# Last stage of a gated decoder layer in two passes, with the output projection by seven block products

## The reference

```python
y_pool = multiscale_pool(u_pool, pool_w[l], pool_scale[l]) * jax.nn.silu(z_pool)
...
y_attn = attn.reshape(B, S, ATTN_WIDTH) * jax.nn.silu(z_attn)
gates = jax.nn.sigmoid(gate_logits + b_gate[l]).reshape(B, S, 2, D)
merged = (gates[:, :, 0] * jnp.einsum('bsp,pd->bsd', y_pool, w_pool_up[l])
          + gates[:, :, 1] * jnp.einsum('bsa,ad->bsd', y_attn, w_attn_up[l]))
x = x + jnp.einsum('bsd,de->bse', merged, w_out[l])
...
return rms_norm(x, final_g)
```

## Time and profile before

| what | value |
|---|---|
| median of 3 runs | 1636.92 us (1635.85 to 1638.66) |
| profiled execution, its own time | 1635.96 us |
| its span, first to last instruction | 1634.2 us |
| mean granted TensorE clock | 0.994 of full speed |
| PE, DVE, ACT, POOL busy, share of the span | 97%, 69%, 46%, 55% |
| DMA, mean over the span | 140 GB/s |

### The profile page before, as it was taken

One profiled execution on the slowest core, in us unless ns is written; L12 is line 12 of the kernel. 1 busy time (PEld: TensorE's weight loads), 2 busy tenths in 40 slices (PEclk: granted clock), 3 DMA queues, 4 the chain that ended last, 5 costly groups with the idle time before them and its releaser, 6 DMA issues. The chain is left out here.

```text
span 1634.2 us, 24931 instructions
## 1 busy us (share of the span) xinstructions
PE 1586.9 (97%) x8030; PEld 1321.3 (81%) x8030; DVE 1134.6 (69%) x1554; ACT 755.8 (46%) x1448; POOL 906.3 (55%) x665
## 2 busy tenths in 40 slices
PE   7999999999999999999999999999999899999998
PEld 5877888788888887888887888888887688888886
DVE  7745425764989889998998988999887763333323
ACT  4422222224667665676665666666666431112111
POOL 3421112421789878888777897898874332314140
PEclk9999999999999999999999999999999999999999
DMA  7742336754434243452793333434314773534332
GB/s 257 233 134 106 129 116 194 250 156 143 140 94 114 82 139 86 114 139 76 242 334 104 107 97 102 119 91 140 100 43 142 220 228 111 165 108 149 116 103 77
DMA packets 150868, 228.82 MB, mean 140 GB/s; under 512 B 46929, under 2 KB 72017, under 8 KB 150754
## 3 DMA queue, kind: packets, MB, share of 16 engines
q1 hardware_dynamic: 150754, 227.42, 45.3%
HBM read 149.76 MB, written 77.60 MB: 139 GB/s over the span
## 5 line engine op out<-in xcount | busy, mean ns | idle before, releaser
L1593 DVE TENSOR_TENSOR_SCAN left<-keep,left 128x512 f32<-128x512 f32 x192 | 297.1, 1547 | 33.5 <-issue 22.4
L1420 PE MATMUL psum<-hT,ring 128*128 128x512 f32 x644 | 264.5, 411 | 5.2 <-DVE sum_d L1629 2.3
L1660 POOL TENSOR_TENSOR ring<-raw,ring 128x512 fp32r<-128x512 f32 x138 | 232.9, 1688 | 60.2 <-ACT ring L1500 45.7
L1424 PE MATMUL psum<-hT,ring 128*128 128x512 f32 x644 | 263.2, 409 | 0.0
L1422 PE MATMUL psum<-hT,ring 128*128 128x512 f32 x644 | 262.6, 408 | 0.0
L1506 ACT ACTIVATE keep<-psum 128x512 f32<-128x512 f32 (+3 forms) x320 | 170.5, 533 | 178.5 <-PE psum L1446 176.5
L1513 ACT ACTIVATE wt<-psum 128x512 fp32r<-128x512 f32 (+3 forms) x320 | 170.9, 534 | 110.8 <-PE psum L1454 107.9
L1466 PEld LDWEIGHTS psum<-wt,vm 128*128 128x128 f32 x1088 | 171.6, 189 | 32.8 <-issue 7.0
L1599 DVE TENSOR_TENSOR wt<-psum,wt 128x512 fp32r<-128x512 f32 (+3 forms) x320 | 189.7, 593 | 8.4 <-ACT wt L1513 5.9
L1466 PE MATMUL psum<-wt,vm 128*128 128x256 f32 x1088 | 182.5, 282 | 5.1 <-DVE row_sum L1608 4.3
L1454 PE MATMUL psum<-ident,left 128*128 128x128 f32 x1088 | 170.8, 272 | 1.4 <-DVE wt L1599 1.3
(11 more groups left out here) (181 smaller groups left out, 3231.3 us busy)
## 6 DMA issues: line engine op xcount, KB each, us to landing
raw<-in_w_strips SPq DMA_DIRECT2D x92, 256.0 KB, 4.1
qm<-qk_scratch SPq DMA_DIRECT2D x128, 128.0 KB, 4.1
gate<-gate_scratch SPq DMA_DIRECT2D x64, 256.0 KB, 4.0
hT<-form_scratch SPq DMA_DIRECT2D x28, 512.0 KB, 8.1
xt<-in_x SPq DMA_DIRECT2D x16, 512.0 KB, 5.2
xT<-in_x_T SPq DMA_DIRECT2D x16, 512.0 KB, 4.1
qk_scratch<-staging SPq DMA_DIRECT2D x32, 256.0 KB, 2.7
qk_scratch<-store_lo SPq DMA_DIRECT2D x32, 256.0 KB, 3.6
```

What stands on the lines that cost most here:

```text
L1420: pe.matmul(o, hi, m_hi, start=k == 0, stop=False)
L1424: last = pe.matmul(o, lo, m_hi, start=False, stop=k == HK - 1)
L1593: dve.tensor_tensor_scan(left[:, n % LN, span][:, ::-1], k, k, carry, ALU.mult, ALU.bypass).then_inc(scanned, 1)
L1660: pool.tensor_tensor(out_, a, b, op).then_inc(s, 1)
```

## The change

Stage 4 is written anew, without hardware loops. It has two passes.

**Pass one** makes the 64 up-projections (`UPS`), for each chunk first the 8 tiles of the pooling branch, then the 8 of the attention branch. The gated pooling tile goes to `rows`, where the attention tile is added, and the sum is stored to a new DRAM scratch, `m_d`. Gate tiles have three buffers (`GN`), and a step n issues the load for step n + 2, which waits until the buffer of step n - 1 is free. Weight pieces have three slots and are now only those of the up-projections, pool's first. The output projection's weights are loaded in the second and third chunk; from their four quarters B11, B12, B21, B22 VectorE forms the sums T1 to T4, and every one of the seven factors (`FORMS`) is split in two parts.

**Pass two** takes the merged values back in 8 pairs of 128 tokens (256 tokens each, `OUT_PAIRS`), in two halves of the channels. Per pair GpSimd forms S1 to S4 (`make_forms`), ScalarE and VectorE split the seven factors into a ring of six, and PE makes seven products of 128 tokens by 512 output channels with 4 slices each (`out_part`, 12 matmuls). The results are put together from PSUM: two by copies on ScalarE, five by adds on VectorE, and six further adds on GpSimd (`join`) in SBUF. x is loaded straight into `rows`, and rows are normed and stored as before.

Two waits of stage 2 on VectorE and GpSimd are also named otherwise or dropped. The diff, cut to its core:

```diff
@@ class Opening @@
-    SLOTS, EARLY = 4, 3
+    SLOTS, EARLY = 3, 3
...
+        b, m = divmod(i, KT)
+        slot = self.raw[:, i % self.SLOTS, :].rearrange("p (k n) -> p k n", n=P)
+        sp.dma_start(slot, self.up[b][:, :, m * P:(m + 1) * P]).then_inc(self.raw_in[i % self.SLOTS], DMA)
@@ build @@
+    m_d = scratch("merged_scratch", [KT, P, SEQ])
@@ stage2 @@
-                                      hT[:, HOME[TURN[i]], kk, 0, :].bitcast(F32), ALU.subtract).then_inc(near_lo, 1)
+                                      hT[:, HOME[TURN[i]], kk, 0, :].bitcast(F32), ALU.subtract)
@@ stage4 @@
-            with pe.Fori(0, NC) as c:
...
-                for m, b in [(0, 0), (1, 0), (0, 1), (1, 1)] + [(m, b) for m in range(2, NM) for b in range(2)]:
-                    up(c, m, b)
...
-                for t in range(1, NT):
-                    for h in range(2):
-                        project(c, t, h, range(KT))
+    NM, UPS = KT, NC * 2 * KT
+    GN, RN, BANKS, AHEAD = 3, 6, 4, 5
+    OUT_PAIRS, PARTS = TT // 2, TT // 2 * FORMS
...
+    def up_of(n):
+        return n // (2 * NM), n // NM % 2, n % NM
+    def at_up(c, b, m):
+        return (2 * c + b) * NM + m
...
+    Y1_TURN = {3: 0, 4: 1, 6: 2, 7: 3}
...
         @block.sync
...
+            def load_gate(n):
+                c, b, m = up_of(n)
+                if n >= GN:
+                    c0, b0, m0 = up_of(n - GN)
+                    if b0 == 0:
+                        sp.wait_ge(gated, n - GN + 1)
+                    else:
+                        sp.wait_ge(summed, c0 * NM + m0 + 1)
+                sp.dma_start(gates[n % GN][:, :], gate_d[b * KT + m, :, tokens(c)]).then_inc(g_in[n % GN], DMA)
...
+            def load_mt(p):
+                if p % 2 == 0:
+                    for i in range(2):
+                        sp.wait_ge(m_stored[i], m_count(p // 2, NM - 2 + i))
+                if p == 0:
+                    sp.wait_ge(w_lo, wo_split(HK, 0))
+                    sp.wait_ge(wo_formed, 4 * HK)
+                    sp.wait_ge(y_lo_done[1], UK * NC)
+                elif p == 1:
+                    sp.wait_ge(up_done, UPS)
+                else:
+                    sp.wait_ge(s_lo, FORMS * (p - 1))
+                for kh in range(2):
+                    sp.dma_start(mt[p % 2][kh][:, :, :], m_d[kh * HK:(kh + 1) * HK, :, pair_tokens(p)].rearrange("k q t -> q k t")
+                                 ).then_inc(mt_in[p % 2], DMA)
...
+            load_gate(0)
             last_stores(sp)
+            load_gate(1)
+            for n in range(UPS):
+                c, b, m = up_of(n)
+                if n + EARLY < 2 * NM:
+                    load_up(n + EARLY)
+                if n + 2 < UPS:
+                    load_gate(n + 2)
+                if n == 4:
+                    load_z(0, 2)
+                    load_z(0, 3)
+                    for s, count in zip(sum_stored, SUM_STORES):
+                        sp.wait_ge(s, count * DMA)
+                    for s in y_stored:
+                        sp.wait_ge(s, PAIRS * 4 * DMA)
+                if m == 0 and b == 1 and c + 1 < NC:
+                    sp.wait_ge(up_done, at_up(c, 1, 0))
+                    opening.load_y(sp, 0, tokens(c + 1))
+                if m == 0 and b == 0 and c >= 1:
+                    sp.wait_ge(up_done, at_up(c, 0, 0))
+                    opening.load_y(sp, 1, tokens(c))
+                    load_z(c, 0)
+                    load_z(c, 1)
+                if m == 4 and b == 0 and c >= 1:
+                    load_z(c, 2)
+                    load_z(c, 3)
+                if n >= 1 and up_of(n - 1)[1] == 1:
+                    store_m(up_of(n - 1)[0], up_of(n - 1)[2])
+                if n >= WO_FIRST - 1 and (n - WO_FIRST + 1) % WO_STEPS == 0 and (n - WO_FIRST + 1) // WO_STEPS < HK:
+                    load_wo((n - WO_FIRST + 1) // WO_STEPS)
+                if n == LATE_FIRST + 1:
+                    load_mt(0)
+                if n >= UPS - 2:
+                    load_x(0, n - UPS + 2)
+            store_m(NC - 1, NM - 1)
+            load_mt(1)
...
+            for p in range(OUT_PAIRS):
+                if p + 2 < OUT_PAIRS:
+                    load_mt(p + 2)
+                for a in range(2):
+                    store(p, a)
+                if p + 2 < OUT_PAIRS:
+                    load_x(p + 2, 0)
+                    load_x(p + 2, 1)
...
         @block.tensor
...
+            def up(n):
+                c, b, m = up_of(n)
+                if c == 0:
+                    pe.wait_ge(w_lo, up_split(b * NM + m))
+                if n >= BANKS:
+                    pe.wait_ge(gated, n - BANKS + 1)
+                cols = slice(m * P, (m + 1) * P)
                 for k in range(UK):
                     if m == 0:
+                        pe.wait_ge(y_lo_done[b], UK * c + k + 1)
+                    last = split3(pe, bank(n), up_hi[b][:, k, cols], up_lo[b][:, k, cols],
                                   y_hi[b][:, k, :], y_lo[b][:, k, :], k == 0, k == UK - 1)
+                last.then_inc(up_done, 1)
...
+            def out_part(s):
+                j = s % FORMS
+                wait_bank(pe, s)
+                pe.wait_ge(s_lo, s + 1)
+                if s < FORMS:
+                    if j in LATE:
+                        pe.wait_ge(w_lo, late_split(HK * LATE.index(j) + HK - 1))
+                    else:
+                        pe.wait_ge(w_lo, wo_split(HK, 0))
+                for k in range(HK):
+                    last = split3(pe, bank(s), ring[:, s % RN, 0, k, :], ring[:, s % RN, 1, k, :],
+                                  form[j][:, k, 0, :], form[j][:, k, 1, :], k == 0, k == HK - 1)
+                last.then_inc(part_done, 1)
+            for n in range(UPS):
...
+            for n in range(UPS):
+                up(n)
+            for s in range(PARTS):
+                out_part(s)
...
         @block.scalar
...
+            for s in range(PARTS + 4):
+                p, j = divmod(s, FORMS)
+                if s < PARTS and j in (A11, S1):
+                    take(s)
+                if s + AHEAD < PARTS:
+                    form_high(s + AHEAD)
+                if p >= 1 and j in (0, 1):
+                    square(p - 1, j)
+                if p >= 1 and j in (1, 2):
+                    root(p - 1, j - 1)
...
         @block.vector
...
+            def apply_gate(n):
+                c, b, m = up_of(n)
+                g = gates[n % GN]
+                dve.wait_ge(g_in[n % GN], (n // GN + 1) * DMA)
+                dve.wait_ge(up_done, n + 1)
+                if b == 0:
+                    if c >= 1:
+                        dve.wait_ge(m_stored[m % 2], m_count(c - 1, m))
+                    dve.tensor_tensor(rows[:, m, :], bank(n), g[:, :], ALU.mult).then_inc(gated, 1)
+                else:
+                    dve.tensor_tensor(g[:, :], bank(n), g[:, :], ALU.mult).then_inc(gated, 1)
...
+            for s in range(PARTS + 4):
+                p, j = divmod(s, FORMS)
+                if s < PARTS and j not in (A11, S1):
+                    add_part(s)
+                if s + AHEAD < PARTS:
+                    form_low(s + AHEAD)
+                if p >= 1 and j in (1, 2):
+                    row_mean(p - 1, j - 1)
+                if p >= 1 and j in (2, 3):
+                    finish_row(p - 1, j - 2)
...
         @block.gpsimd
...
             def merge(c, m):
+                n = at_up(c, 1, m)
+                pool.wait_ge(gated, n + 1)
+                pool.tensor_tensor(rows[:, m, :], rows[:, m, :], gates[n % GN][:, :], ALU.add).then_inc(summed, 1)
...
+            def make_forms(w):
+                p, j = divmod(w, FORMS)
+                a11, a12, a22, s1, s2, s3, s4 = (form_tile(p, i) for i in (A11, A12, A22, S1, S2, S3, S4))
+                if j == A11:
+                    pool.wait_ge(mt_in[p % 2], (p // 2 + 1) * 2 * DMA)
+                    if p >= 2:
+                        pool.wait_ge(s_lo, FORMS * (p - 1))
+                    pool.tensor_tensor(s3, a11, s3, ALU.subtract).then_inc(s_formed, 1)
+                    pool.wait_ge(s_formed, 4 * p + 1)
+                    pool.tensor_tensor(s2, a22, s3, ALU.subtract).then_inc(s_formed, 1)
+                if j == A12:
+                    pool.wait_ge(s_formed, 4 * p + 2)
+                    pool.wait_ge(s_lo, FORMS * p + A11 + 1)
+                    pool.tensor_tensor(s1, s2, a11, ALU.add).then_inc(s_formed, 1)
+                if j == S2:
+                    pool.wait_ge(s_lo, FORMS * p + A12 + 1)
+                    pool.tensor_tensor(s4, a12, s2, ALU.subtract).then_inc(s_formed, 1)
...
+            for s in range(PARTS):
+                p, j = divmod(s, FORMS)
+                if j == A11:
+                    join(p, 1)
+                if j == S2:
+                    join(p, 2)
+                if j == S1:
+                    join(p, 3)
+                if j == S3:
+                    join(p, 4)
+                    join(p, 5)
```

(4 more changed lines are left out.)

691 lines of the change are left out of this document (380 added, 311 removed).

## The result

| | before | changed |
|---|---|---|
| median | 1637.58 us (6 runs, 1635.84 to 1638.66) | 1643.70 us (6 runs, 1641.34 to 1645.31) |
| profiled execution, its span | 1634.2 us | 1641.4 us |
| mean granted clock | 0.994 | 0.988 |

The ratio is 1.0040, 95% interval 1.0027 to 1.0052: the change makes the kernel **slower by 0.4%**, where I had forecast 1613.5 us and faster. The 1643.7 us lie outside my range.

What follows compares the result with a forecast made beforehand. PE was taken as the bound: 1269.2 + 1439 x 0.2268 = 1595.6 us, plus 6.0 losses, 10.0 end and 1.8 around the span gave 1613.4, stated as 1613.5 us; range 1606 to 1625.

Steps and rivals of the forecast that it cites:

- 96 matmuls less, -21.8 us: Output projection: 672 matmuls in place of 768, at 0.2268 us each, all of it saved on PE's path.
- The opening, 2 us: Start of pass one: attention-half weight pieces come late behind gate loads in SP's queue; 2 us lost, between nothing and 8.8.
- The attention tiles, 1.5 us: Pass one: a chunk's last attention tile is late when z lands in 8.4 us; 0.7 us in three chunks, 1.5 taken.
- Half clock and seams, 1.5 us: Both passes: slower first matmuls of each group and stretches at the lower clock cost 1.5 us.
- Pass two, 1 us: All eight output pairs: PE's 19.05 us per pair holds, with 1 us lost in all; ends 0 and 10.
- stretching brings DVE to 16.6 us: Pass two: GpSimd lengthens nine DVE operations by 0.44 us each, giving 16.6 of PE's 19.05 us per pair.
- short lateness is covered by 8 to 10 us: Pass two: factors filled five products ahead and four banks cover short lateness by 8 to 10 us.
- The tail, 10.0 us: After the last matmul's start: the last rows' norms run one after the other, +1.9 us, making 10.0 us.
- The lock's 20.3 us a pair: Rival, pass two: DVE and POOL work at SBUF takes strict turns, 20.3 us a pair, 1623 us; chance 0.14.
- its own sign: The lock's sign in pass two: pairs longer than 19.05 us with DVE or POOL without a gap.
- The ring: Rival, pass one: three gate buffers turn too slowly, 1652 us; chances 0.08 for 1616 to 1635, 0.05 over 7.6 us landing.
- sign rival: The gate-buffer rival of pass one: kernel slower than before if landings average over 7.6 us; 1652 us, chance 0.05.

Runs made afterwards that it cites:

- e17_psum_rows: e14_third_rows with ScalarE multiplying rows by their scale into PSUM and VectorE multiplying that by the gain, one step later still; 1618.6 us, ratio 0.9896.
- e9_pieces: The change with four z tiles (two behind the gate load), y load earlier, row scalings later, output weights two steps later, up-projection pieces one step earlier; 1636.4 us.
- e1_four_z: The change with four z tiles in place of two, loaded together; 1637.7 us, ratio 1.0002.
- e2_y_first: The change with the load of y moved in front of that step's gate load in SP's order; 1642.0 us, ratio 1.0026.
- e19_pass_two: The change with e17_psum_rows' edits of pass two alone: third row buffers, mt and x loaded earlier, scaling through PSUM; 1635.3 us, ratio 0.9981.
- e16: e14_third_rows without the final row scaling of 1016 of 1024 columns; 1619.9 us, one run.
- e18: e14_third_rows with the row scalings one more step later on VectorE, still in SBUF; 1624.7 us, ratio 0.9917.
- e14_third_rows: e11_all with a third pair of row buffers in pass two, so x is loaded a whole pair ahead; 1628.5 us, ratio 0.9954.
- e12_all_wolate: e11_all with the output weights split one up-projection step later on ScalarE and VectorE; 1635.9 us, ratio 0.9984.
- e11_all: The change with four z tiles, y load earlier, up-projection pieces earlier, row scalings one step later and merged values (mt) loaded a pair earlier; 1630.7 us, ratio 0.9957.
- e6: The change with the two row scalings one product later in VectorE's order, behind sum_d; 1649.4 us, ratio 1.0080.
- e3: The change with row scaling in two steps: ScalarE multiplies by the scale into PSUM, VectorE multiplies that by the gain; 1652.4 us, ratio 1.0095.

## Why the prediction was wrong

- **96 matmuls less, -21.8 us.** Held: 768 and 672 matmuls ran at 0.2268 us. e17_psum_rows shows that the work is really saved, once nothing waits.
- **The opening, 2 us.** The mechanism was right, and the term 1.2 us too small. PE waited twice for a piece of the attention half, 3.2 us, and e9_pieces takes both waits away.
- **The attention tiles, 1.5 us: the step that failed first.** The prediction says "The last attention tile of a chunk is ready with 1 to 2 us to spare by my walk", and charges only what one landing takes longer, 0.7 us in each of three chunks. Measured are 10.9 us of waits in place of 1.5. Two z buffers make the second pair of tiles wait for the first pair's low parts, and these for y: two landings follow each other, of 8.0 to 8.8 and of 4.5 to 5.5 us. e1_four_z takes these waits away. In front of that, y is issued 5.2 us behind its free buffer, since three gate loads in SP's queue wait for GpSimd's sums. What this delay costs by itself stays open, since e2_y_first shortens it by only 0.8 us. I had charged each load its landing, and not the chain of issue, landing, product, issue, landing.
- **Half clock and seams, 1.5 us.** 5.4 us of steps at 0.43 us and 2.6 us of others in pass one, and 0.7 in pass two. I had seen the link between a long wait and the slow steps and had no long waits to apply it to: once the waits were mispriced, so was this.
- **Pass two, 1 us: the second failure.** 8.4 us. That stretching brings DVE to 16.6 us was nearly right (17.2 measured). The step that failed is "short lateness is covered by 8 to 10 us": the cover is one of stock, and a loop that turns more slowly than PE uses it up. Two pairs at 19.04 us, one at 19.21, then 20.7 each. I had added up each engine's work and asked whether it exceeds 19.05 us, but had not followed the order of sum_d, joins and row scalings round the loop. e19_pass_two, with that loop and the two over SP opened and the scaling taken through PSUM, has pairs of 19.04 us and is 8.4 us under the change.
- **The tail, 10.0 us.** 12.3 us. GpSimd's fifth and sixth join stand between the last matmul and the last square, and I had counted only the norms. With these sizes the sum comes out: 33.6 us of losses for 6.0 and 12.3 of end for 10.0 make 1643.4 us.
- **The rivals.** The lock's 20.3 us a pair comes near the 20.7, but its own sign did not appear: neither engine was without a gap. The time in which at least one of them did excluding work, from the starts and ends of those instructions, was 18.4 of 20.7 us. The low parts averaged 1307 ns (those from `mt`), but PE waited for adds and for no low part. Yet the lock has its share, since it lengthens VectorE's work in the loop, as e16, e17 and e18 show. The page "SBUF — State Buffer" of the Trainium skill (section "Who interferes with whom") says that the other engine is fully blocked. This trace agrees for operations with two SBUF inputs (1.28 to 2.40 us for one scaled row) but for a short overlap: in e14_third_rows 29.3 us of such work fill 18.2 us, the waiting counted in. The ring did not turn too slowly: gates landed in 3.8 us from 1300 to 1340 us, and PE waited 0.8 us for a gate product. Its sum was also a little high: the named parts give L + 2.4 and L + 1.1 us, which makes 1648 us and not 1652. My sign rival was thus the wrong one; the loss came through the y and z loads in the same queue.

What stays open: why e12_all_wolate lost 5 us to e11_all in pass one. Its weights' steps meet other gate products, but I have not tried each alone. Pass one of e17_psum_rows still takes 11.3 us more than its 174.2, 6.0 of them in waits for gate products.

## What to carry to other kernels

Where engines run in written order and depend on each other, add up not only each engine's work but each loop: start at one instruction, follow order and waits through engines and queues until the same instruction of the next round, and compare that length with the bound engine's time. Opening one loop alone can make it slower (e6), as can a step added to one (e3). PE's own pace came back only with three loops opened and the scaling taken through PSUM; which of these could be left out I have not tried. And where VectorE and GpSimd both work in SBUF, count the time an instruction is held up as VectorE's own, and take what can come from PSUM out of it.
